# First group's up products as seven products of quarters, with weight sums kept in DRAM

## The chip, the cores and the metric

The kernel runs on one core of a Trainium2 chip. The metric is the device time of one execution in microseconds. TensorE (PE in the profile) multiplies, VectorE (DVE), ScalarE (ACT) and GpSimd (POOL) do the elementwise work, and SyncE (SP) issues most of the DMAs. Each engine runs its own instruction list in order; they wait for each other by semaphores (`x.wait_ge(sem, n)`, `.then_inc(sem, k)`). SBUF and PSUM tensors have 128 partitions.

## The reference

One inference step of a one-layer decoder, in fp32: 1024 prompt tokens with 16 meta tokens ahead of them, and 8 sequences of 8 new tokens over 8192 cached ones (1104 rows in all). Two branches run side by side, an RWKV-7 recurrence and sparse attention whose keys an indexer picks (the best 256 per query). Their outputs are gated and projected, and a convolutional FFN follows:

```python
def conv_ffn(h, conv_prev, lp):
    u = h @ lp['w_up']                     # 1024 -> 2 x 2816
    a, b = u[..., :D_FF], u[..., D_FF:]
    ext = jnp.concatenate([conv_prev.astype(a.dtype), a], axis=1)
    c = lp['conv_b'] + ext[:, 0:T] * lp['conv_w'][0]
    for j in range(1, CONV_W):             # CONV_W = 3
        c = c + ext[:, j:j + T] * lp['conv_w'][j]
    y = (jax.nn.gelu(c, approximate=False) * b) @ lp['w_down']
    return y, ext[:, T:]
```

`h` is the RMS-normed row of the residual stream. For the new tokens the indexer's top 256 of 8200 scores per query are needed before their attention can run.

## The kernel before

The program runs in stages: `project_attention` (attention inputs, blocks of 128 rows), `prompt_and_project` (prompt attention beside the RWKV projection), `sample_scores`, the RWKV factors and chunks, and `tail`, in which the change mostly lies. `tail` keeps rows as columns: the 1104 rows are three groups g = 0, 1, 2 of 368 columns (W), with the 1024 features in 8 tiles (KD) of 128 partitions. Each group goes through branch (16 products), project (8), up and down.

*Up and down of groups 0 and 1.* For each of 22 tiles f (NF) of the FFN width, `up(g, f, j)` makes `a` (j = 0) and `b` (j = 1): 8 matmuls each of a 128x128 weight with XN's 368 columns, into three PSUM banks in turn (R0, R1, R2), each given back through `freed`. ScalarE's `read_a` reads `a` with the three taps of the convolution, `read_b` copies `b`; GpSimd adds the taps (`conv_add`), ScalarE does the gelu (`curve`), and GpSimd multiplies by `b` into HT (`gate_up`). Then `down(g, t, h)` makes 8 output tiles t of 22 matmuls each, VectorE's `add_down(g, t)` adds a tile to X1 and frees its bank, ScalarE squares it, and TensorE's `sum_tile` sums the squares over partitions for the next norm. In group 0 `sum_tile(1, t - 1)` stands in TensorE's list right behind `down(0, t, 1)` for t from 1 to 7.

*The norm ahead of group 0's up products.* VectorE writes XN as X1 times the gain only (L2984). The first `a` and `b` are multiplied from it and are scaled afterwards by 1/RMS (`temper`, L2769), while GpSimd scales XN's eight tiles in place (L2629), each once TensorE's first `b` has read it.

*The top-k.* SC holds 4100 scores per partition (two halves of a query's scores in partitions p and p + 64). `topk(i)` is one of 96 steps of VectorE: MAX8, FIND_INDEX8, MATCH_REPLACE8 in turn, 32 rounds of 8. `steps(a, b)` does steps a to b - 1. They are spread through VectorE's list: 0 to 10 in group 0's branch and project, 11 and 12 around the reciprocal and the tempering, 13 to 61 during group 0's up products, 62 to 77 between its `add_down`s, 78 to 95 in group 1.

*The new tokens' attention.* In group 1 `lists()` (VectorE) turns the top-k into cache rows, with small transfers by GpSimd behind block LISTED and LISTED + 1; TensorE flips the list ahead of block FLIP; GpSimd hands `conv_add` over to VectorE from block BY_POOL and starts 128 indirect loads of keys and values into KV; and 36 `slot(s)` pieces of attention run on TensorE, two per up block from F0 on and then three per down tile (at CUTS). SP waits for `summed`, which slot 34 completes, before it loads group 2's branch inputs into YT, which lies in KV's space.

*Group 2* uses another scheme for up and down (`block3`): the weight and the moving tile are cut into quarters (two halves of the contraction, and `a` and `b` of the weight, two halves of 184 columns), and seven products of quarters take the place of eight, Strassen's scheme in Winograd's form. It needs four sums of weight quarters, made by VectorE (`weight_sum`, L1983 to L1989), and four mixtures of quarters of XN (`mix_norm`, L2870 to L2878). The seven results are kept or added by ScalarE, VectorE and GpSimd.

*`project_attention`* works through nine blocks of rows: TensorE 32 matmuls (L148), ScalarE copies with scale (L180), VectorE `rope` (L202 and on) and `level` (L225), SP stores k, v and the index keys (L98).

## Time and profile before

| | us |
|---|---|
| median of three runs (lowest, highest) | 2738.84 (2736.39, 2741.65) |
| the profiled execution: its own time | 2747.19 |
| the profiled execution: span, first to last instruction | 2745.4 |
| TensorE busy in the span | 2612.7 (95%) |
| VectorE busy | 1675.1 (61%) |
| ScalarE busy | 765.2 (28%) |
| GpSimd busy | 331.3 (12%) |
| granted TensorE clock, mean | 0.967 |
| group 0's up products, about | 1475 to 1697 |
| group 0's down products, about | 1697 to 1810 |
| group 1's up and down products, about | 1900 to 2337 |
| group 2's seven-product blocks, from | 2431 |

In the profile PE is TensorE's matmuls and PEld its weight loads, which overlap them; a matmul of this kernel in fp32 is two instructions of each kind. "L2214" is line 2214 of the kernel. Times in the timelines are microseconds from the start of the span; a bracket behind a row is the idle time of the engine in front of it and what ended it. An average over the whole span hides that stages have different limits, so the stages around the change are read one by one.

### The profile page before, as it was taken

The page shows a single profiled execution, that of the slowest core. Times are in us where ns is not written, and L with a number is a line of the kernel's source. Part 1 is how long each engine was busy: PE and PEld are TensorE (multiplying, and loading weights), DVE is VectorE, ACT ScalarE, POOL GpSimd, SP SyncE. Part 2 cuts the span into 40 slices and gives each one's busy share as a digit, 9 for nine tenths or more (in the row PEclk, how much of TensorE's full clock was granted, in tenths as well). Part 3 has the DMA queues.
Part 4 walks back from the last instruction along what each step waited for, and adds up shares of the span by engine and source line. Part 5 has one row for each costly group of instructions (what it writes and reads, how often), then busy time and mean ns, then how long its engine had stood idle before and what let it go on. Part 6 is the DMA issues. An engine that isn't in the chain of part 4 may idle for free.

```text
span 2745.4 us, 47811 instructions
## 1 busy us (share of the span) xinstructions
PE 2612.7 (95%) x18832; PEld 1734.1 (63%) x18832; DVE 1675.1 (61%) x3223; ACT 765.2 (28%) x1624; POOL 331.3 (12%) x467
## 2 busy tenths in 40 slices
PE   8998999999997997899899999999999999999997
PEld 5553566666654323788755666655656666579997
DVE  2115888864533457667669999977853321357666
ACT  2224322125443663011112332012335421222212
POOL 0000111000000000000002222000344440011111
PEclk9999999999998986999899999999999999999999
DMA  6101112131113440000243333344356663433332
GB/s 219 34 13 41 41 67 85 67 101 37 49 49 125 176 145 16 5 26 12 91 131 114 107 107 114 105 149 141 111 175 210 191 206 109 151 126 123 124 123 72
DMA packets 86591, 280.52 MB, mean 102 GB/s; under 512 B 18520, under 2 KB 42936, under 8 KB 72992
## 3 DMA queue, kind: packets, MB, share of 16 engines
q1 hardware_dynamic: 74336, 226.34, 24.7%
q0 software_dynamic: 12032, 51.14, 5.8%
q8 instruction: 149, 2.44, 0.4%
q14 instruction: 74, 0.61, 0.1%
HBM read 244.48 MB, written 32.16 MB: 101 GB/s over the span
## 4 chain that ended last, share of the span: by engine, by line
PE 53%; DVE 3%; issue 1%; DVEq 1%; DMA 1%; ACT 0%; POOL 0%; ACTq 0%; POOLq 0%; SPq 0%
PE banks L2214 10%; PE banks L2253 6%; PE banks L2232 6%; PE tl_P L2214 5%; PE tl_P L2253 4%; PE rc_P L1366 3%; PE tl_P L2232 2%; PE banks L2146 2%; PE banks L2158 2%; PE banks L1378 1%; PE tl_P L2146 1%; PE rc_LV L1378 1%; PE tl_P L2311 1%; PE tl_P L2332 1%; PE tl_P L2158 1%
## 5 line engine op out<-in xcount | busy, mean ns | idle before, releaser
L408 PE MATMUL dp_PS<-base,dp_W 128*128 128x368 f32 x1440 | 465.8, 476 | 0.0
L408 PEld LDWEIGHTS dp_PS<-base,dp_W 128*128 128x128 f32 x1440 | 265.8, 190 | 157.5 <-issue 8.8
L2214 PE MATMUL banks<-base,tl_WU 128*128 128x368 f32 x944 | 299.9, 475 | 0.8 <-DVE base L2763 0.8
L2214 PEld LDWEIGHTS banks<-base,tl_WU 128*128 128x128 f32 x944 | 179.2, 191 | 113.2 <-issue 3.6
L148 PE MATMUL pa_PG<-pa_W,base 128*128 128x402 f32 (+1 forms) x576 | 198.6, 505 | 7.7 <-DMA pa_W<-in_w_dsa 7.7
L707 DVE TENSOR_SCALAR_CACHE_REDUCE dp_EQ<-dp_SCORE,dp_trial 128x1024 f32<-128x1024 f32 (+1 forms) x186 | 176.0, 946 | 19.9 <-issue 1.1
L148 PEld LDWEIGHTS pa_PG<-pa_W,base 128*128 128x128 f32 (+1 forms) x576 | 106.9, 187 | 94.4 <-issue 14.2
L2232 PE MATMUL banks<-base,tl_WD 128*128 128x368 f32 x484 | 153.5, 474 | 0.0
L2214 PE MATMUL tl_P<-base,tl_WU 128*128 128x368 f32 x464 | 151.2, 477 | 0.2
L2704 DVE MAX8 tl_v<-arena 128x8 f32<-128x4100 f32 x32 | 141.8, 4431 | 2.9 <-issue 1.1
L2707 DVE FIND_INDEX8 tl_i<-tl_v,arena 128x8 uint32<-128x4100 f32 x32 | 141.5, 4423 | 0.3 <-issue 0.3
L2710 DVE MATCH_REPLACE8 arena<-tl_v,arena 128x4100 f32<-128x4100 f32 x32 | 141.2, 4414 | 0.0
L2654 POOL DMA_INDIRECT arena<-in_cache_kv,tl_PHT x128 | 123.3, 963 | 110.0 <-PE tl_P L2332 73.9
L2232 PEld LDWEIGHTS banks<-base,tl_WD 128*128 128x128 f32 x484 | 90.8, 190 | 57.2 <-issue 2.9
L2214 PEld LDWEIGHTS tl_P<-base,tl_WU 128*128 128x128 f32 x464 | 87.6, 191 | 58.1 <-POOL base L2629 4.3
L2427 ACT ACTIVATE arena<-base 128x368 f32<-128x368 f32 x44 | 22.1, 509 | 273.1 <-DVEq L2747 109.8
L202 DVE TENSOR_TENSOR pa_t<-pa_H,pa_cs 128x168 f32<-128x168 f32 (+1 forms) x9 | 3.0, 334 | 147.5 <-ACT pa_H L180 147.5
L785 DVE CUSTOM_DVE_ANT_0 dp_P<-dp_PS,dp_SCORE 128x1024 f32<-128x1024 f32 (+7 forms) x64 | 48.5, 758 | 66.7 <-PE dp_PS L458 59.1
L2158 PE MATMUL banks<-base,arena 128*128 128x368 f32 x256 | 81.3, 473 | 2.2 <-issue 1.4
L2146 PE MATMUL banks<-arena 128*128 128x368 f32 x240 | 77.3, 473 | 1.6 <-DMA arena<-in_wb 0.8
L2394 POOL TENSOR_TENSOR base<-tl_T 128x368 f32<-128x368 f32 x34 | 28.7, 843 | 400.9 <-ACTq L2477 400.8
L2232 PE MATMUL tl_P<-base,tl_WD 128*128 128x368 f32 x220 | 69.8, 474 | 0.0
(500 smaller groups left out, 4608.5 us busy)
## 6 DMA issues: line engine op xcount, KB each, us to landing
tl_WU<-in_wu SPq DMA_DIRECT2D x58, 1024.0 KB, 4.9
tl_WD<-in_wd SPq DMA_DIRECT2D x32, 704.0 KB, 4.2
dp_W<-in_w_rw SPq DMA_DIRECT2D x15, 1024.0 KB, 5.1
arena<-in_wb SPq DMA_DIRECT2D x24, 512.0 KB, 3.8
arena<-in_wo SPq DMA_DIRECT2D x24, 512.0 KB, 3.8
gates<-dp_PX SPq DMA_DIRECT2D x16, 552.0 KB, 3.6
arena<-gates SPq DMA_DIRECT2D x48, 184.0 KB, 3.9
arena<-in_wu SPq DMA_DIRECT2D x8, 1024.0 KB, 4.9
```

The source lines that it names most:

```text
L148: last = pe.matmul(PG[0:n, c, 0:NC4], xT[:, k, r:r + n], W[:, c, k, :], start=k == 0, stop=k == KD - 1)
L408: last = pe.matmul(bank(f)[:, 0:w], W[:, t // 2 % 2, k, 128 * (t % 2):128 * (t % 2) + 128], xT[:, k, c:c + w], start=k == 0, stop=k == KD - 1)
L707: dve.tensor_scalar(EQ[0:n, 0:m], scored_of(j), values(n, x), None, op, ALU.add, accum_out=result[0:n, x:x + 1])
L2146: last = pe.matmul(out[:, 0:W], WM[:, i % 2, o:o + 128], YT[:, j, k, :], start=k == 0, stop=k == 3)
L2158: last = pe.matmul(out[:, 0:W], WM[:, i % 2, 128 * k:128 * k + 128], MT[:, k, :], start=k == 0, stop=k == KD - 1)
L2214: last = pe.matmul(out[:, 0:W], WU[:, i % 2, o:o + 128], XN[:, k, :], start=k == 0, stop=k == KD - 1)
L2232: last = pe.matmul(out[:, 0:W], WD[:, i % 3, 128 * e:128 * e + 128], HT[:, f, :], start=f == 0, stop=f == NF - 1)
L2253: last = pe.matmul(out[:, 0:H], weights[:, k, :], moving(k), start=first and k == 0, stop=k == kk - 1, skip_group_check=True)
L2654: pool.indirect_dma_start(out=KV[:, n % 16, t, :], out_offset=None, in_=I["cache_kv"], in_offset=bass.IndirectOffsetOnAxis(ap=PHT[:, 64 * ...
L2704: dve.max(v8[:, :], SC)
L2707: dve.max_index(i8[:, :], v8[:, :], SC)
L2710: dve.match_replace(SC, v8[:, :], SC, TAKEN)
```

## The change

*In `project_attention`* SP loads each of the 22 up weights (1 MB), VectorE makes the four sums of its quarters in one to three tiles per row block, and SP writes them to a DRAM tensor `wsum` (1 MB per tile). ScalarE's squares are written over their input, which frees the room of `junk`.

*In group 0* only tile f = 0 is still made by `up`. Tiles 1 to 21 are made by `up_block(f)`: seven products of four matmuls of 184 columns into banks FA, FB, FD and FE, with weights from WU and, newly loaded for each tile, from WF (the sums out of `wsum`). ScalarE copies each result out of its bank (`keep`), seven per tile, and applies the taps from AF in SBUF; GpSimd makes the five additions between the parts and still does `conv_add` and `gate_up`. VectorE scales XN's low four tiles, GpSimd the high four; VectorE makes the four mixtures (XF) and only then does `steps(11, 62)`, where steps 11 and 12 were ahead of or between the reciprocal and the temperings.

*In group 1* BY_POOL, LISTED, FLIP and F0 are each two blocks later, so that 12 slots run in the up and 24 in the down products, and `sums` of the third norm waits for the last slot. Buffers, semaphore counts and the order of banks are adapted.

```diff
+                    for f in ups_of(b):
+                        sp.wait_ge(pair_summed, f + 1)
+                        sp.dma_start(wsum[f], WS[:, f % 2].rearrange("p e n -> p (e n)")).then_inc(ws_out[f % 2], 16)
+                        if f + 2 < NF:
+                            load_up(f + 2)
...
+                def sum_up(f):
+                    q, s = WQ[:, f % 2], WS[:, f % 2]
+                    dve.wait_ge(wq_in[f % 2], 16 * (f // 2 + 1))
+                    if f >= 2:
+                        dve.wait_ge(ws_out[f % 2], 16 * (f // 2))
+                    dve.tensor_tensor(s[:, 0], q[:, 2], q[:, 3], ALU.add)
+                    dve.tensor_tensor(s[:, 2], q[:, 0], q[:, 2], ALU.subtract)
+                    dve.drain()
+                    dve.tensor_tensor(s[:, 1], s[:, 0], q[:, 0], ALU.subtract)
+                    dve.drain()
+                    dve.tensor_tensor(s[:, 3], q[:, 1], s[:, 1], ALU.subtract)
+                    dve.drain().then_inc(pair_summed, 1)
...
                     if b:
                         level(b - 1)
+                    for f in ups_of(b):
+                        sum_up(f)
                 level(NB - 1)
...
-BY_POOL, LISTED, FLIP, F0 = 12, 3, 12, 14
+BY_POOL, LISTED, FLIP, F0 = 14, 5, 14, 16
...
                 order += [("rows", g - 1, i) for i in range(6)]
             if g < 2:
-                order += [(x, g, f) for f in range(NF) for x in "ab"] + [("down", g, t) for t in range(KD)]
+                order += [(x, g, f) for f in range(NF if g else 1) for x in "ab"] + [("down", g, t) for t in range(KD)]
...
-                    if i >= 2:
-                        sp.wait_ge(b_done, i - 1)
+                    if i == 2:
+                        sp.wait_ge(b_done, 1)
+                    elif 2 < i < NF + 2:
+                        sp.wait_ge(fd_made, 2 * (i - 2))
+                    elif i >= NF + 2:
+                        sp.wait_ge(b_done, i - NF)
                     sp.dma_start(WU[:, i % 2, :], I["wu"][:, i % NF]).then_inc(wu_in[i % 2], 16)
...
+                def load_sums(f):
+                    if f == 1:
+                        sp.wait_ge(branched, 16)
+                        sp.wait_ge(merged, 16)
+                    if f >= 3:
+                        sp.wait_ge(fd_made, 2 * (f - 2))
+                    sp.dma_start(WF[:, f % 2].rearrange("p e k m -> p (e k m)"), wsum[f]).then_inc(wf_in[f % 2], 16)
...
+                    if g == 0:
+                        load_sums(1)
+                        load_sums(2)
...
+                            if g == 0 and f >= 3:
+                                load_sums(f)
...
+                    if n == 3:
+                        pe.wait_ge(y_done, TS // 4)
...
-                        if j == 0 and f == (1 if g == 0 else 0):
+                        if j == 0 and f == 0 and g:
...
+                    def product(out, weights, moving, first):
+                        for k in range(4):
+                            if f == 1 and moving is left:
+                                pe.wait_ge(xn_done, 2 * k + 2)
+                            last = pe.matmul(out[:, 0:H], weights[:, k, :], moving(k), start=first and k == 0,
+                                             stop=k == 3, skip_group_check=True)
+                        return last
...
+                    def second():
+                        pe.wait_ge(fb_taken, 2 * f - 2)
+                        if f == 1:
+                            pe.wait_ge(xf_done, 2)
+                        product(FB, ws[:, 1], lambda k: XF[:, 1, k, :], True).then_inc(fb_made, 1)
...
+                    left = lambda k: XN[:, k, half[0]]
+                    pe.wait_ge(wu_in[f % 2], 16 * (f // 2 + 1))
+                    pe.wait_ge(wf_in[f % 2], 16 * ((f + 1) // 2))
+                    pe.wait_ge(fa_taken, 2 * f - 2)
+                    product(FA, raw[:, 0], left, True).then_inc(fa_made, 1)
+                    if f > 1:
+                        second()
+                    pe.wait_ge(fd_taken, 2 * f - 2)
...
+                    product(FD, ws[:, 0], lambda k: XF[:, 0, k, :], True).then_inc(fd_made, 1)
+                    if f == 1:
+                        pe.wait_ge(freed[FREED_B], uses0[FREED_B])
+                        second()
+                    pe.wait_ge(fa_taken, 2 * f - 1)
+                    if f == 1:
+                        pe.wait_ge(xn_high, 4)
+                    product(FA, raw[:, 1], lambda k: XN[:, 4 + k, half[0]], False).then_inc(fa_made, 1)
+                    if f == 1:
+                        pe.wait_ge(xf_done, 4)
+                    pe.wait_ge(fb_taken, 2 * f - 1)
+                    product(FB, ws[:, 2], lambda k: XF[:, 2, k, :], False).then_inc(fb_made, 1)
+                    pe.wait_ge(fe_taken, f - 1)
+                    product(FE, raw[:, 3], lambda k: XF[:, 3, k, :], True).then_inc(fe_made, 1)
+                    pe.wait_ge(fd_taken, 2 * f - 1)
+                    product(FD, ws[:, 3], lambda k: XN[:, 4 + k, half[1]], False).then_inc(fd_made, 1)
...
-                    for f in range(NF):
+                    if g == 0:
+                        up(0, 0, 0)
+                        up(0, 0, 1)
+                        pe.wait_ge(freed[FREED_A], uses0[FREED_A])
+                        for f in range(1, NF):
+                            up_block(f)
+                        pe.wait_ge(fa_taken, 2 * NF - 2)
+                        pe.wait_ge(fb_taken, 2 * NF - 2)
+                        pe.wait_ge(fd_taken, 2 * NF - 2)
+                        pe.wait_ge(fe_taken, NF - 1)
+                    for f in range(NF if g else 0):
...
+                def keep(part, bank, made, taken, count):
+                    act.wait_ge(made, count)
+                    act.activation(part, bank[:, 0:H], ACT.Copy).then_inc(taken, 1)
...
+                def taps(f):
+                    s = f % 2
+                    w0, w1, w2, cb = (cw[:, k, f:f + 1] for k in range(4))
+                    if f >= 2:
+                        act.wait_ge(convolved, f - 1)
+                    act.wait_ge(f_right, f)
...
+                    act.activation(T[:, s, 0, 0:W], AF[:, s, 0:W], ACT.Identity, bias=cb, scale=w0)
...
+                    act.activation(AL[:, f, :], AF[:, s, W:W + 2], ACT.Copy)
+                    act.drain().then_inc(a_read, 1)
+
+                def keep_block(f):
+                    s = f % 2
+                    if f >= 3:
+                        act.wait_ge(b_read, f - 1)
+                    keep(f1[:, s, :], FA, fa_made, fa_taken, 2 * f - 1)
+                    if f > 1:
+                        taps(f - 1)
+                    keep(f6[:, s, :], FB, fb_made, fb_taken, 2 * f - 1)
+                    keep(f5[:, s, :], FD, fd_made, fd_taken, 2 * f - 1)
+                    keep(AF[:, s, 2:2 + H], FA, fa_made, fa_taken, 2 * f)
+                    keep(f7[:, s, :], FB, fb_made, fb_taken, 2 * f)
+                    curve(0, f - 1)
+                    keep(f4[:, s, :], FE, fe_made, fe_taken, f)
+                    keep(f3[:, s, :], FD, fd_made, fd_taken, 2 * f)
...
-                for k in range(KD):
+                for k in range(4, KD):
                     if k < KD - 1:
                         pool.wait_ge(gain_read, k + 1)
                     else:
                         pool.wait_ge(b_done, 1)
-                    pool.tensor_tensor(XN[:, k, :], XN[:, k, :], RS[:, :], ALU.mult).then_inc(xn_done, 1)
-                for f in range(NF):
-                    conv_add(pool, 0, f)
-                    if f:
-                        gate_up(pool, 0, f - 1)
+                    pool.tensor_tensor(XN[:, k, :], XN[:, k, :], RS[:, :], ALU.mult).then_inc(xn_high, 1)
+                def finish_up(f):
+                    s = f % 2
+                    pool.wait_ge(fd_taken, 2 * f)
+                    pool.tensor_tensor(AF[:, s, 2 + H:2 + W], f16[:, s, :], f3[:, s, :], ALU.add).then_inc(f_right, 1)
+                    pool.tensor_tensor(BC[:, s, half[1]], f167[:, s, :], f5[:, s, :], ALU.add)
+                    pool.wait_ge(fe_taken, f)
+                    pool.tensor_tensor(BC[:, s, half[0]], f167[:, s, :], f4[:, s, :], ALU.add)
+                    pool.drain().then_inc(b_read, 1)
+
+                for f in range(1, NF):
+                    s = f % 2
+                    if f > 1:
+                        finish_up(f - 1)
+                    pool.wait_ge(fa_taken, 2 * f - 1)
+                    pool.wait_ge(fb_taken, 2 * f - 1)
+                    pool.tensor_tensor(f16[:, s, :], f1[:, s, :], f6[:, s, :], ALU.add)
+                    conv_add(pool, 0, f - 1)
+                    gate_up(pool, 0, f - 1)
+                    pool.wait_ge(fb_taken, 2 * f)
+                    pool.tensor_tensor(f167[:, s, :], f1[:, s, :], f7[:, s, :], ALU.add)
+                    pool.drain()
+                finish_up(NF - 1)
+                conv_add(pool, 0, NF - 1)
...
-                    dve.tensor_tensor(TX[:, 2], high[:, :, half[1]], low[:, :, half[1]], ALU.subtract).then_inc(tx_done, 1)
+                    if first_group:
+                        temper("b", b_done)
+                        dve.wait_ge(xn_high, 4)
+                    dve.tensor_tensor(to[:, 1], high[:, :, half[1]], to[:, 0], ALU.subtract).then_inc(done, 1)
+                    dve.tensor_tensor(to[:, 2], high[:, :, half[1]], low[:, :, half[1]], ALU.subtract).then_inc(done, 1)
                     dve.drain()
-                    dve.tensor_tensor(TX[:, 3], high[:, :, half[0]], TX[:, 1], ALU.subtract).then_inc(tx_done, 1)
+                    dve.tensor_tensor(to[:, 3], high[:, :, half[0]], to[:, 1], ALU.subtract).then_inc(done, 1)
...
                     if g == 0:
-                        steps(11, 12)
                         dve.wait_ge(rooted, 1)
                         dve.reciprocal(RS[:, :], RS[:, :])
                         dve.drain().then_inc(inverted0, 1)
                         temper("a", a_done)
-                        steps(12, 13)
-                        temper("b", b_done)
-                        steps(13, 62)
+                        for k in range(4):
+                            dve.wait_ge(gain_read, k + 1)
+                            dve.tensor_tensor(XN[:, k, :], XN[:, k, :], RS[:, :], ALU.mult).then_inc(xn_done, 2)
+                        mix_rows(XF, xf_done, True)
+                        steps(11, 62)
```

## Rows read from the trace of the kernel before

**Rows 1.** The profile's page, part 4: the chain by engine.

```profile
PE 53%; DVE 3%; issue 1%; DVEq 1%; DMA 1%; ACT 0%; POOL 0%; ACTq 0%; POOLq 0%; SPq 0%
```

**Rows 2.** Busy us of PE, PEld, DVE, ACT, POOL; clock; DMA share, GB/s.

```profile
1475.00:1697.00 222.00, 221.64 (x711) 134.06 (x710) 217.83 (x116) 72.90 (x179) 65.91 (x73) 1.00 0.30 105
```

**Rows 3.** Groups by line, VectorE, 1483 to 1697 (busy us, mean ns).

```profile
L2704 DVE MAX8 tl_v<-arena 128x8 f32<-128x4100 f32 x16 | 70.9, 4432 | 1.1
```

**Rows 4.** Timelines of TensorE and VectorE (start us, us, engine line operation).

```profile
1696.75 13.77 PE L2232 MATMUL tl_P<-base,tl_WD 128*128 128x368 f32 x44
...
1739.08 13.77 PE L2232 MATMUL tl_P<-base,tl_WD 128*128 128x368 f32 x44
...
1717.86 0.54 DVE L2746 TENSOR_TENSOR base<-base,tl_P 128x368 f32<-128x368 f32 x1
...
1737.13 0.54 DVE L2746 TENSOR_TENSOR base<-base,banks 128x368 f32<-128x368 f32 x1
```

**Rows 5.** Chain that ended last, in order of time (start us, us).

```profile
1494.10 9.89 PE banks L2214 x32
...
2441.86 2.49 PE tl_P L2253 x16
```

**Rows 6.** Timelines of TensorE and GpSimd at the head of the up products.

```profile
1479.34 7.58 PE L2214 MATMUL banks<-base,tl_WU 128*128 128x368 f32 x24
1486.86 7.25 PE L2214 MATMUL tl_P<-base,tl_WU 128*128 128x368 f32 x16
...
1485.75 7.41 POOL L2629 TENSOR_TENSOR base<-base,tl_RS 128x368 f32<-128x368 f32 x8 [90.57 <-PE banks L2214]
```

**Rows 7.** Timeline of VectorE at the same place.

```profile
1478.54 4.41 DVE L2710 MATCH_REPLACE8 arena<-tl_v,arena 128x4100 f32<-128x4100 f32 x1
...
1483.19 2.45 DVE L2997 RECIPROCAL tl_RS<-tl_RS 128x368 f32<-128x368 f32 x1
...
1490.72 0.55 DVE L2769 TENSOR_TENSOR banks<-banks,tl_RS 128x368 f32<-128x368 f32 x1
```

**Rows 8.** Timeline of VectorE, last group's mixtures.

```profile
2433.18 0.93 DVE L2875 TENSOR_TENSOR arena<-base,arena 128x736 f32<-128x736 f32 x1
...
2435.04 0.93 DVE L2878 TENSOR_TENSOR arena<-base,arena 128x736 f32<-128x736 f32 x1
```

**Rows 9.** Timelines of VectorE and GpSimd in the second group.

```profile
2008.55 1.10 DVE L2798 TENSOR_TENSOR arena<-arena 128x128 f32<-128x128 f32 x1
...
2012.25 0.29 DVE L2798 TENSOR_TENSOR arena<-arena 128x128 f32<-128x128 f32 x1
...
2008.54 0.96 POOL L2396 TENSOR_TENSOR base<-base,tl_T 128x368 f32<-128x368 f32 x1
```

**Rows 10.** Busy time and clock (columns as rows 2), and TensorE's timeline.

```profile
2044.00:2046.00 2.00, 2.00 (x7) 1.48 (x6) 0.00 (x0) 1.55 (x4) 1.63 (x2) 0.50 0.97 385
...
2043.13 1.88 PE L2311 MATMUL tl_P<-ident,arena 128*128 128x128 f32 x8 [2.61 <-DMA arena<-in_cache_kv,tl_PHT]
2044.80 6.02 PE L2214 MATMUL tl_P<-base,tl_WU 128*128 128x368 f32 x16
```

**Rows 11.** Groups by line and form, last group, 2430 to 2600.

```profile
L1985 DVE TENSOR_TENSOR arena<-arena,tl_WU 128x512 f32<-128x512 f32 x13 | 9.0, 692 | 1.2
...
L2682 POOL TENSOR_TENSOR base<-arena 128x184 f32<-128x184 f32 x14 | 8.0, 573 | 121.7 <-DVE arena L2926 121.7
...
L2524 ACT ACTIVATE arena<-banks 128x184 f32<-128x184 f32 x19 | 6.0, 318 | 27.0 <-PE banks L2253 26.7
```

**Rows 12.** DMA issues, 1475 to 1697 and 2300 to 2420 (KB, us to landing).

```profile
tl_WU<-in_wu SPq DMA_DIRECT2D x20, 1024.0 KB, 4.8
tl_WD<-in_wd SPq DMA_DIRECT2D x3, 704.0 KB, 7.4
...
arena<-ya_dram SPq DMA_DIRECT2D x1, 608.0 KB, 7.5
```

**Rows 13.** Timeline of VectorE in the attention projection.

```profile
101.78 0.33 DVE L202 TENSOR_TENSOR pa_t<-pa_H,pa_cs 128x168 f32<-128x168 f32 x1 [19.14 <-ACT pa_H L180]
```

More of the change, by code:

```diff
@@ L1963, in tail @@
         uses = [sum(1 for n in use.values() if n % 3 == r) for r in range(3)]
+        uses0 = [sum(1 for n in use.values() if n % 3 == r and n <= use["b", 0, 0]) for r in range(3)]
         NBL = len(BLOCKS3)
@@ L3131, in program @@
                         ident)
[L3132 removed]
+        tail(nc, I, S, M, soon, gates, wsum, yr_dram, ya_dram, O["v"], O["conv"], O["y"], ident)
 def shape_constants():
```

74 lines of the change are left out of this document (54 added, 20 removed).

## The prediction, made before the changed kernel was built or run

> **What bounds the kernel now.** I read the chain of waits first, then the busy time by stretch, then each engine's timeline at the ends of that stretch. The chain names TensorE for most of the run [rows 1], and in the first group's up products (1475 to 1697) TensorE is busy 221.64 of 222 us, so that the stage looks like pure TensorE work. In the same row VectorE is busy 217.83 of 222 us [rows 2]. That is the top-k over the 4100 scores per partition: each of its 96 steps is one search of 4.4 us [rows 3]. The reader should see what these steps stand in front of. In VectorE's program steps 13 to 61 come ahead of `add_down(0, 0)` (L2743). TensorE's own waits are: `sum_tile(1, t - 1)` after each down tile t waits for the square of tile t - 1, and that waits for `add_down`. In the trace the first down product starts at 1696.75 and is done 13.6 us later, but its addition starts only at 1717.86, directly behind a search; the second starts at 1737.13, again behind searches, with its tile done at about 1724. TensorE starts down tile 3 at 1739.08 [rows 4], 1.95 us after that second addition, once its square and the sum of it are done. By its own pace (13.6 us a down tile of 22 matmuls, 0.62 us a sum of squares) it would have started 0.1 us sooner. So before the change the two engines arrive at this point together. From tile 3 on TensorE sets the pace (14.22 us a tile) and VectorE waits for it. The start of down tile 3 is the gate, and the time at which it opens is the later of two chains: TensorE's (up products, three down tiles, a sum) and VectorE's (51 search steps, two additions, four more search steps).
>
> **TensorE's chain gets shorter.** An up block is two products of 8 matmuls of 368 columns, 32 instructions (a matmul is two of them) in 9.89 us. The last group already has the seven-product block: 16 of its instructions, of 184 columns, take 2.49 us, and a block has 7 x 8 = 56 of them, 8.72 us [rows 5]. 21 blocks change: 21 x (9.89 - 8.72) = 24.6 us. Head and end: before, the second block waits about 2.1 us for GpSimd's scalings (7.25 us for 16 instructions that take 5.1 with the tail of the last) [rows 6]; after, it waits about 1.3 us for the second mixture and 0.5 us for the last banks to be kept. Sum: 24.9 us, so the up products end at about 1671.9 instead of 1696.75.
>
> **VectorE's chain gets longer.** Before, VectorE does step 11 (from 1478.5 to 1483.19), the reciprocal (2.45 us), the tempering of the first `a`, step 12, the tempering of `b` at 1490.72, and starts step 13 at 1491.2 [rows 7]. After, steps 11 and 12 move behind the new work. Their price: step 11 4.7 us, step 12 4.5 us (a search of 4.43 us [rows 3] and its overhead), together 9.2 us. The new work fills the place that they had, and a little more. Sums 6 and 7 of the squares do not move, so the root is ready near 1480.5; reciprocal to 1483.0; tempering `a` to 1483.5; four scalings at 0.46 to 0.55 us, the last not before 1484.3, when TensorE has read tile 3, end at 1485.0. Then mixture 0, a TENSOR_TENSOR of 128x736, 0.93 us [rows 8]. The next step must wait: mixture 1 needs the high half of XN, which GpSimd scales tile by tile behind TensorE's reads of `b` (tile 4 is read at 1484.95, tile 7 at 1486.86 [rows 6]). GpSimd's eight such scalings now take 7.41 us, 0.93 each [rows 6], so its four end at 1488.6 if nothing disturbs them. Three mixtures of 0.85 to 1.0 us follow: 2.8 us (from the second to the end of the fourth [rows 8]). Step 11 would start at 1491.5.
>
> One more term. A VectorE operation with two tensors in SBUF beside a GpSimd operation takes up to its partner's time more: the same 128x128 addition takes 0.29 us alone and 1.10 us at 2008.55, while a GpSimd addition runs [rows 9]. Mixture 0 and GpSimd's first scaling start within 0.1 us of each other, so I add one GpSimd operation, 0.9 us, bounds 0 and 1.9. Step 11 starts at 1492.5. The shift of the search chain is then 1492.5 + 9.2 - 1491.2 = 10.5 us, with bounds 9.6 and 11.5. The searches themselves (one input tensor) I leave at 4.43 us although GpSimd gets five more additions a block: 16 of them beside GpSimd's present work average 4432 ns [rows 3].
>
> [...]
>
> **Which chain wins.** TensorE now ends its second down tile at 1671.9 + 27.2 = 1699.1 and must stand still until the first addition, 1717.86 + 10.5 = 1728.4, has been squared: about 30 us idle. It finishes tile 2 near 1744 and waits again for the second addition, 1737.13 + 10.5 = 1747.6. The gate opens at 1739.08 + 10.5 = 1749.6. All of the 24.9 us are spent waiting, and 10.5 us are lost on top. What is late next is everything behind it, one to one, as TensorE is busy without a gap from there.
>
> **The clock.** In the second group TensorE waits 2.61 us for the first gathered keys. Behind that wait its granted clock is 0.50, the 1.2 GHz level, from 2044 to 2046, and the 16 instructions from 2044.80 take 6.02 us where such 16 take 5.1 [rows 10]. With the slow transposes ahead of them that wait cost some 1.5 us beyond its own length. The 30 us idle will do the same, but what it costs falls into the 4 to 5 us of slack ahead of the gate. The second wait, 2 to 5 us, stands right at the gate. I take 1.5 us for it, bounds 0 and 3.
>
> The Trainium skill, "TensorE: Matmul & The Clock Gate", Part 1, says that the array is throttled by default and that activity lifts it, so that idle time is paid for after it ends. The row from 2044 agrees. Without that rule my sum would be 1.5 us less.
>
> **What is hidden, and by what.** (1) The block's other engines have to keep TensorE's pitch only loosely: three down tiles and a sum before 1749.6 allow the up stage to last until about 1708, 10.4 us a block against 8.72. ScalarE per block: seven keeps of 0.32 us [rows 11], the taps and the gelu, some 5 us. GpSimd: five additions of 0.57 us [rows 11] beside its present three (0.84 to 0.97), 5.6 us. Each block now loads two times 1 MB; one lands in 4.8 us, three of 704 KB together in 7.4 us [rows 12]. All are below 8.7. (2) Attention projection: 22 sums of four TENSOR_TENSORs of 128x512 at 0.69 us [rows 11], three sums a block, 8.4 us, in a hole of 19.1 us [rows 13]. The third sum waits for a load that is issued after the first: about 3.8 + 7.4 + 2.8 = 14 us after the hole opens, 5 us before it closes. Cost nothing; if the cover were gone, TensorE's `turn` of each block would come late by the excess. On SP a block's output writes stay ahead of its sums, and the row load behind them has a block and more in hand. (3) Second group: list, flip and slots come two blocks later. GpSimd no longer stands at its list transfers until the last search is done, VectorE waits for those transfers instead, and the flip is two blocks, 19.8 us, later, so TensorE does not feel it. The 36 attention slots cost TensorE the same in the down stage as in the up stage. (4) The last slots end some 9.5 us (15 matmuls of 0.62 us) ahead of the end of the down stage. SP waits for slot 34 before it loads the branch inputs; the last of these needs 7.5 us [rows 12] and is issued 2 us after the first, just in time. Cost 0, bounds 0 and 4 us.
>
> **Sum.** +10.5 (VectorE's chain) + 1.5 (clock) = +12 us. The profiled execution spans 2745.4 us and took 2747.19; it would become 2759.2. It stands 8.35 us above the median of the runs shown, 2738.84, so the forecast for the median is 2750.8 us.
>
> **Rivals.** *TensorE sets the end* (the searches turn out not to stand in the way): then the gain comes through, 2738.84 - 24.9 = 2714 us. For it: the chain names TensorE everywhere [rows 1]. Against it: the additions at 1717.86 and 1737.13 stand directly behind searches [rows 4]. It would need VectorE to be 25 us earlier. Chance 0.07. *The block's ring is slower than 10.4 us*: a keep, an addition and a load that don't overlap as I think. It decides from 10.4 us a block on; at 11 us the gate opens 21 x 0.6 = 13 us later still, 2764 us. For it: keeps and taps are in one queue with crossed waits. Against: 5 and 5.6 us of work in 8.7. Chance 0.07. *The third weight sum overruns its hole*: if the write and the load together need 6 us more than I take, 1 us a block in 7 blocks and more; at 3 us a block, 21 us, 2772 us. Chance 0.04. *The chains cancel*: the added wait is as computed, but fewer idle microseconds elsewhere (the slots meet more cover in the down stage, the 2.61 us wait goes) give back 7 to 12 us; about 2741 us. Against: TensorE is busy without gaps in that stage. Chance 0.09. *My forecast*: 0.73.
>
> **How the numbers follow.** The forecast's own range is 2738.84 + 9 to + 19 us (lower: 9.6 with no clock loss and 0.6 us for the spread of a median; upper: 11.5 + 3 + 4), 2748 to 2758. For 8 in 10 I add the near halves of the cancelling case and of the slow ring: 2743 to 2762 us. A measurement tells 0.2%, 5.5 us, from no change. Faster 0.08, same 0.10, slower 0.82.
>
> **What would show it.** The first `add_down` of group 0 about 10 us later than 1717.86, with a search right in front of it; a TensorE gap of about 30 us behind the second down tile and a short one behind the third; up blocks every 8.7 us; step 11 starting near 1492; no gap longer than today's in the attention projection; the distance from down tile 3 to the end as before. An up stage that is short and a first addition that is no later than 1718 would prove me wrong, and so would up blocks over 10.4 us.

## The result

The changed kernel takes 2756.85 us (median of four runs, 2755.63 to 2758.95), the kernel before 2738.26 us beside it: ratio 1.0060, 95% interval 1.0047 to 1.0073. The two medians differ by 18.6 us; the ratio gives 16.4 us (12.9 to 20.0). On a second occasion the ratio was 1.0055 (1.0042 to 1.0068). The mean of the two is 1.0057, +15.7 us. The forecast was +12 us, 2750.8, with a range of 2743 to 2762.

The profiled execution of the changed kernel spans 2755.2 us. That is only 9.8 us more than the span of before, since before's profiled execution lay 8.9 us above its median and this one lies at its median. Two single executions are therefore not compared by their ends here, but stage by stage.

The page of the changed kernel, busy time of each engine and the chain by engine (part 1 and part 4):

```profile
PE 2587.2 (94%) x19336; PEld 1784.8 (65%) x19336; DVE 1738.1 (63%) x3313; ACT 786.1 (29%) x1704; POOL 390.5 (14%) x575
...
PE 43%; DVE 10%; DVEq 4%; issue 1%; DMA 1%; ACT 0%; POOL 0%; ACTq 0%; POOLq 0%; SPq 0%
```

TensorE has 25.5 us less to do, and the run is longer. The chain answers [rows 1]: there PE held 53% of the span and DVE 3%, now PE holds 43% and DVE 10%. VectorE's new share is the search chain of the first group, which the chain now follows from 1493 to 1731. Its busy time by stretch (columns: PE, PEld, DVE, ACT, POOL busy, clock, DMA share, GB/s) answers [rows 2]:

```profile
1478.00:1673.00 195.00, 193.31 (x1206) 188.68 (x1205) 187.10 (x105) 96.80 (x258) 116.89 (x169) 1.00 0.60 227
1673.00:1752.00 79.00, 45.16 (x138) 26.89 (x137) 77.32 (x43) 3.62 (x8) 4.84 (x7) 0.81 0.17 51
```

The up products end at 1673, and in the 79 us behind them TensorE is busy for 45 while VectorE is busy for 77. TensorE's timeline at the gate (start us, us, then the idle time before and what ended it), with VectorE's first two additions of the group, answers [rows 4]:

```profile
1673.89 13.84 PE L2292 MATMUL tl_P<-base,tl_WD 128*128 128x368 f32 x44 [0.57 <-issue]
1687.57 13.77 PE L2292 MATMUL banks<-base,tl_WD 128*128 128x368 f32 x44
1732.34 1.59 PE L2177 MATMUL tl_P<-arena,tl_ones 128*128 128x368 f32 x2 [31.00 <-ACT arena L2543]
1733.72 15.61 PE L2292 MATMUL banks<-base,tl_WD 128*128 128x368 f32 x44
1751.61 0.89 PE L2177 MATMUL tl_P<-arena,tl_ones 128*128 128x368 f32 x2 [2.27 <-ACT arena L2543]
1752.33 13.77 PE L2292 MATMUL tl_P<-base,tl_WD 128*128 128x368 f32 x44
...
1726.62 4.42 DVE L2881 FIND_INDEX8 tl_i<-tl_v,arena 128x8 uint32<-128x4100 f32 x1
1731.11 0.54 DVE L2920 TENSOR_TENSOR base<-base,tl_P 128x368 f32<-128x368 f32 x1
...
1750.38 0.54 DVE L2920 TENSOR_TENSOR base<-base,banks 128x368 f32<-128x368 f32 x1
```

TensorE stands still for 31.00 us behind its second down tile. The wait is booked to ScalarE's square (L2543), but that square waits for the addition at 1731.11, and the addition stands directly behind a search. All three times of [rows 4] are 13.25 us later: the first addition, the second and down tile 3 (1739.08 before, 1752.33 now).

### The profile page after: what moved, and what is told of

The parts are those of the page before. It is cut to its first block, busy times and chain, and to the rows that moved or that the text cites. A ratio compares the mean times of both kernels' runs of the same rounds, so it can differ in the third digit from the quotient of the medians.

```text
span 2755.2 us, 49283 instructions
## 1 busy us (share of the span) xinstructions
PE 2587.2 (94%) x19336; PEld 1784.8 (65%) x19336; DVE 1738.1 (63%) x3313; ACT 786.1 (29%) x1704; POOL 390.5 (14%) x575
## 4 chain that ended last, share of the span: by engine, by line
PE 43%; DVE 10%; DVEq 4%; issue 1%; DMA 1%; ACT 0%; POOL 0%; ACTq 0%; POOLq 0%; SPq 0%
PE banks L2359 6%; PE banks L2274 5%; PE banks L2292 5%; PE tl_P L2359 4%; DVE arena L2884 3%; DVE tl_v L2878 3%; DVEq L2882 3%; PE rc_P L1395 3%; PE tl_P L2274 2%; PE banks L2206 2%; PE banks L2218 2%; PE tl_P L2292 2%; PE banks L1407 1%; PE tl_P L2206 1%; PE tl_P L2417 1%
## 5 line engine op out<-in xcount | busy, mean ns | idle before, releaser
L162 PEld LDWEIGHTS pa_PG<-pa_W,base 128*128 128x128 f32 (+1 forms) x576 | 107.2, 187 | 94.7 <-issue 14.3
L2274 PE MATMUL banks<-base,tl_WU 128*128 128x368 f32 x496 | 158.8, 477 | 0.8 <-DVE base L2937 0.8
L2878 DVE MAX8 tl_v<-arena 128x8 f32<-128x4100 f32 x32 | 141.8, 4432 | 3.3 <-issue 1.5
L2274 PEld LDWEIGHTS banks<-base,tl_WU 128*128 128x128 f32 x496 | 94.4, 192 | 60.0 <-issue 3.6
L2543 ACT ACTIVATE arena<-base 128x368 f32<-128x368 f32 x44 | 22.1, 509 | 295.7 <-DVEq L2921 143.2
L2304 PE MATMUL banks<-arena 128*128 128x184 f32 x504 | 85.6, 319 | 1.4 <-DVE arena L3052 1.4
L2304 PEld LDWEIGHTS banks<-arena 128*128 128x128 f32 x504 | 80.0, 190 | 1.6 <-issue 1.6
L2274 PE MATMUL tl_P<-base,tl_WU 128*128 128x368 f32 x240 | 76.8, 473 | 0.0
L594 ACT ACTIVATE dp_PMT<-dp_PS,dp_rest 128x368 f32<-128x368 f32 x42 | 23.8, 568 | 164.8 <-PE dp_PS L437 164.8
```

Source lines behind the costliest of these rows:

```text
L162: last = pe.matmul(PG[0:n, c, 0:NC4], xT[:, k, r:r + n], W[:, c, k, :], start=k == 0, stop=k == KD - 1)
L2274: last = pe.matmul(out[:, 0:W], WU[:, i % 2, o:o + 128], XN[:, k, :], start=k == 0, stop=k == KD - 1)
L2304: last = pe.matmul(out[:, 0:H], weights[:, k, :], moving(k), start=first and k == 0, stop=k == 3, skip_group_check=True)
L2878: dve.max(v8[:, :], SC)
```

## The experiments

The kernels ran on five occasions, and the kernel before, which ran on each, took 2738.3, 2768.3, 2767.0, 2742.7 and 2763.4 us on them. So kernels of different occasions are compared only by their ratios to the kernel before. For the stages I use marks on VectorE, the reciprocals of the norms ahead of group 0's up products (A), behind its down products (B), ahead of group 1's up products (C) and behind its down products (D). A to B is the stage of the change. A to B and B to C hardly depend on the occasion (329.66 and 329.67 for the kernel before on two of them); C to D does.

| kernel | ratio (95%) | A to B | B to C | C to D |
|---|---|---|---|---|
| before | 1 | 329.66 | 82.44 | 445.04 |
| `before_again` | 1.0001 (0.9989 to 1.0013) | 329.67 | 82.44 | 468.63 |
| `before_2_more` | 1.0032 (1.0018 to 1.0046) | 338.24 | 82.44 | 465.62 |
| `before_12_fewer` | 0.9992 (0.9982 to 1.0003) | 329.40 | 82.44 | 444.90 |
| `sums_alone` | 0.9999 (0.9987 to 1.0011) | 330.44 | 82.44 | 468.48 |
| `later_lists_alone` | 0.9995 (0.9982 to 1.0007) | 329.68 | 82.44 | 467.30 |
| after | 1.0060 (1.0047 to 1.0073) | 344.66 | 82.44 | 443.39 |
| `after_again` | 1.0055 (1.0042 to 1.0068) | 343.99 | 82.45 | 465.55 |
| `after_3_fewer` | 1.0006 (0.9996 to 1.0017) | 330.71 | 82.44 | 468.72 |
| `after_12_fewer` | 0.9929 (0.9915 to 0.9942) | 308.21 | 82.43 | 467.27 |
| `after_sums_postponed` | 1.0003 (0.9993 to 1.0013) | 331.63 | 82.43 | 467.47 |
| `moved_searches` | 0.9945 (0.9928 to 0.9961) | 310.23 | 85.89 | 444.30 |
| `moved_postponed` | 0.9941 (0.9925 to 0.9957) | 308.06 | 85.89 | 443.32 |
| `moved_searches_2` | 0.9934 (0.9919 to 0.9948) | 308.93 | 82.44 | 469.36 |

(The reciprocal A itself stands 2.7 us earlier in the changed kernel, counted from TensorE's sum in front of it, since step 11 is no longer in front of it; so the 15.0 us from 329.66 to 344.66 are 12.3 us of later work.)

**Theory and rivals.** Theory: the gate is set by VectorE's search chain, and what TensorE saves is spent waiting at it. Rivals: the sums in the attention projection cost what the gate leaves open; the later lists and slots cost time; the up blocks of quarters are slow; TensorE sets the pace and the searches are cover.

**One part of the change alone.** `sums_alone` is the kernel before with the new `project_attention`, whose sums nobody reads:

```diff
-            project_attention(nc, I, xT, ident, T, O["k"], O["v"], O["ki"], S)
+            project_attention(nc, I, xT, ident, T, O["k"], O["v"], O["ki"], wsum)
```

> The kernel before with only the weight sums in the attention projection (loads, four VectorE operations per tile, writes); nobody reads them. My theory: they lie in VectorE's hole of 19 us per block, so +1 us (the trace of after is 0.7 us late at the end of that stage), 2738 to 2741 us. Rival, that the sums are the unexplained part of the change: the medians differ by 18.6 us, of which the later gate explains about 13, so that 5 to 9 us come from here: 2743 to 2747 us.

The ratio says -0.3 us, with an interval from -3.6 to +3.0. The rival of 5 to 9 us is out. The traces resolve smaller differences than that. One of the softmax reciprocals of the prompt attention, always the same one, stands at 860.12, 860.09, 860.08, 861.12 and 860.19 in the five kernels without the sums (mean 860.3), and between 861.38 and 863.06 in the nine with them (mean 862.3). So the kernels with the sums are some 2 us late by then, where I had 0. VectorE's timeline of a row block of the changed kernel shows that the hole itself holds as computed:

```profile
105.14 1.22 DVE L239 TENSOR_TENSOR base<-base,pa_PR 128x1024 f32<-128x1024 f32 x1
106.55 0.69 DVE L248 TENSOR_TENSOR pa_WS<-pa_WQ 128x512 f32<-128x512 f32 x1 [0.19 <-issue]
...
118.44 0.69 DVE L248 TENSOR_TENSOR pa_WS<-pa_WQ 128x512 f32<-128x512 f32 x1 [6.04 <-DMA pa_WQ<-in_wu]
...
125.52 0.33 DVE L216 TENSOR_TENSOR pa_t<-pa_H,pa_cs 128x168 f32<-128x168 f32 x1 [4.25 <-ACT pa_H L194]
```

The third sum waits 6.04 us for its load, and 4.25 us of waiting for ScalarE are still left in front of `rope` (L216). The 2 us are not in the blocks: TensorE starts the next stage at 223.97 on average with the sums and at 223.73 without (224.27 and 223.57 in the first traces). The rest comes up behind that, in three steps. About 1.0 us of it goes back to this place, in the timelines of VectorE, GpSimd and TensorE of the changed kernel:

```profile
503.79 2.04 DVE L755 TENSOR_SCALAR dp_step<-dp_count 128x7 int32<-128x7 f32 x1
...
503.78 2.03 POOL L685 TENSOR_TENSOR dp_PMT<-dp_PMT,dp_PX 128x1040 f32<-128x1040 f32 x1 [12.63 <-ACTq L603]
...
590.73 1.56 PE L487 MATMUL dp_PS<-base,QT 64*128 64x512 f32 x6 [1.59 <-DVEq L819]
```

In the kernel before, the same operation of 128x7 elements starts 0.5 us ahead of the GpSimd addition and takes 0.17 us, and the wait at the third row is 0.59 us. In all nine kernels with the sums, one of the small operations at this place (L755 or L757) starts with or just behind the addition and takes 1.83 to 2.04 us; of the five without them only `before_2_more` has it (2.03 us), and it is the one at 861.12. The other two steps are 0.35 us each: VectorE has short "issue" gaps in this stage (seven of 0.4 to 0.5 us, 3.1 us in all, in `before`; nine, 4.1 us, in `after`), and in the kernels with the sums they stand at other instructions of its list, two of them where TensorE waits for it. This is read from the 14 traces; no run was made to separate it.

`later_lists_alone` is the kernel before with the constants and the norm's wait:

```diff
-BY_POOL, LISTED, FLIP, F0 = 12, 3, 12, 14
+BY_POOL, LISTED, FLIP, F0 = 14, 5, 14, 16
...
+                    if n == 3:
+                        pe.wait_ge(y_done, TS // 4)
```

> The kernel before with only the four constants (list, flip, hand-over of conv_add and slots two blocks later) and the third norm's wait for the last slot. My theory: TensorE's work is the same and the pieces of attention cost the same beside up as beside down: 0, at most -2 us. Rival, that slots moved from the up to the down products or the later end of the slots cost time: +3 us and more (the branch inputs of the third group come late by up to 4 us).

-1.4 us (-5.0 to +1.9), and its stage C to D is 1.3 us shorter than that of `before_again`. After is 1.65 us shorter than before in the same stage. The price of 0 (at most -2) holds, and the rival is out.

**The kernel before again.** This run changes nothing.

> The kernel before, unchanged, as a kernel of its own: ratio 1.000. It tells what its profiled execution is worth: the one shown spans 2745.4 us, about 9 us more than its median allows. If that span was one slow execution, this one spans about 2736 to 2738; if the profile itself stretches this kernel, it spans 2745 again.

The ratio fits (1.0001), but neither expectation of the span does: the kernel before now takes 2768 us, and its span is 2766.7. A to C is as before, and C to D is 23.6 us longer. TensorE's timeline shows where (start us, us, idle time before):

```profile
2058.40 0.47 PE L2214 MATMUL banks<-base,tl_WU 128*128 128x368 f32 x1 [1.63 <-issue]
2059.83 0.47 PE L2214 MATMUL banks<-base,tl_WU 128*128 128x368 f32 x1 [0.96 <-issue]
2063.32 0.77 PE L2214 MATMUL banks<-base,tl_WU 128*128 128x368 f32 x1 [3.03 <-issue]
2065.42 0.77 PE L2214 MATMUL banks<-base,tl_WU 128*128 128x368 f32 x1 [1.33 <-issue]
```

For 19 us TensorE issues single matmuls with 0.4 to 3 us of "issue" between them, 15.3 us in all; over the whole stage the granted clock is at its 1.2 GHz level for 31 us, against 7 us in the first trace of before. The gaps start 26 us after GpSimd's first indirect load (22 to 28 us in the nine traces that have them). The kernels of three of the four later occasions have it, changed or not, and those of the fourth (`moved_searches`, `moved_postponed`, `before_12_fewer`) don't, nor do the first traces of before and after. So it belongs to the occasion and cancels in the ratios. As for the 8.9 us by which before's first profiled execution lay over its median, this run only shows that its own profiled execution lies at its median, with runs between 2762 and 2773. The cause of the 8.9 us stays open.

**VectorE's chain alone, in the kernel before.**

```diff
                     if i % 3 == 0:
+                        if i in (24, 27):
+                            dve.max(v8[:, :], SC)
+                            dve.drain()
                         dve.max(v8[:, :], SC)
```

> The kernel before with two more MAX8 searches (their results are those of the searches behind them) among the steps of the first group's up products, so that only VectorE's chain grows, by 2 x 4.6 = 9.2 us, and TensorE's work is the same. My theory: both chains arrive together before the change (TensorE 0.1 us sooner), so the time grows by the whole of it: +9 us, 2747. Rival, TensorE sets the pace there and the searches are cover: 0.

+8.9 us by the ratio (5.0 to 12.7), +8.57 by stage A to B. TensorE's work is that of before, and it waits in the same place as in the changed kernel:

```profile
1724.73 1.59 PE L2119 MATMUL tl_P<-arena,tl_ones 128*128 128x368 f32 x2 [3.52 <-ACT arena L2427]
1726.12 16.07 PE L2232 MATMUL banks<-base,tl_WD 128*128 128x368 f32 x44
1744.00 0.89 PE L2119 MATMUL tl_P<-arena,tl_ones 128*128 128x368 f32 x2 [1.81 <-ACT arena L2427]
1744.72 13.77 PE L2232 MATMUL tl_P<-base,tl_WD 128*128 128x368 f32 x44
```

The counterpart takes 54 us out of VectorE's chain, with this in `topk` (r is the round; steps 24 to 35):

```diff
+                    if 8 <= r < 12:
+                        if i % 3 == 2:
+                            dve.tensor_copy(VAL[:, 8 * r:8 * r + 8], v8[:, :])
+                            dve.tensor_copy(IDX[:, 8 * r:8 * r + 8], i8[:, :])
+                            dve.drain()
```

> The kernel before with four rounds of the top-k (steps 24 to 35) left out in the first group's up products, copies of the round before in their place. My theory: before the change TensorE's chain is only 0.1 us ahead of VectorE's at the gate, so taking 54 us from VectorE gives 0 to -2 us. Rival, the searches bounded the kernel before as well: -10 us and more.

-2.2 us (-4.9 to +0.8), and -0.26 in stage A to B. So before the change both chains arrive together: 9 us more of searches cost 9, 54 us less give almost nothing. TensorE's own pace would open the gate 0.26 us sooner, for 0.1 in the prediction (whose own rates, three tiles of 13.6 us and two sums of 0.62 us from 1696.75, give 1738.8, 0.3 us sooner).

**The changed kernel with a shorter search chain.** The same lines, for one round and for four; like `before_12_fewer`, these kernels leave out part of the top-k.

> The changed kernel as it is, beside the kernel before on this chip, on which the kernel before takes 2768 us: ratio 1.0068 (+18.6 us) if the whole of the measured difference belongs to the change; 1.0045 (+12.4 us), if the gate (down tile 3 starts 12.3 us later, less the 1 us that was there ahead of the stage, and at most 2 us elsewhere) is all of it.

> The changed kernel with one round of the top-k (steps 24 to 26: MAX8, FIND_INDEX8, MATCH_REPLACE8) left out in the first group's up products; the round's eight results are copies of the round before, so part of the top-k isn't computed. My theory: VectorE's chain sets the gate, so 13.5 us less than the changed kernel (3 x 4.6 us less 0.3 us for the copies that stay), the first addition at 1717.6 and down tile 3 at 1738.8. Rival, the up blocks of quarters, their copies or loads are what costs: no change, the same time as the changed kernel.

> The changed kernel with four rounds (steps 24 to 35, 54 us of VectorE) left out in the same way. My theory: from some 36 us on TensorE sets the pace again, so down tile 3 starts at about 1716.4 (down products from 1673.9, three tiles of 13.8 and two sums) instead of 1752.3, and the time is 36 us below the changed kernel, about 23 us below the kernel before; the rest of the 54 us becomes VectorE's waiting. If VectorE were the limit all along, -54 us; if it never was, 0.

Against `after_again`, which ran beside them, one round less gives 1.0055 - 1.0006 = 0.0049 of 2767 us, 13.6 us, and 13.3 in stage A to B; expected 13.5. Four rounds less give 34.9 us by the ratios and 35.8 in the stage; expected 36. In the latter TensorE runs through the gate at its own pace (sum at 1695.29, 27.3 us behind the first down tile, where the changed kernel has 58.4):

```profile
1668.00 13.84 PE L2292 MATMUL tl_P<-base,tl_WD 128*128 128x368 f32 x44 [0.57 <-issue]
1681.68 13.77 PE L2292 MATMUL banks<-base,tl_WD 128*128 128x368 f32 x44
1695.29 0.78 PE L2177 MATMUL tl_P<-arena,tl_ones 128*128 128x368 f32 x2
...
1710.13 13.77 PE L2292 MATMUL tl_P<-base,tl_WD 128*128 128x368 f32 x44
```

Against the kernel before, this stage is 21.45 us shorter, and 24.2 us with the 2.7 us by which A stands earlier. That is the saving on TensorE which the changed kernel does not get out: the up blocks are not slow.

**The wait itself.** VectorE's work stays, TensorE asks for the addition one tile later:

```diff
-                        if g == 0 and t >= 1:
-                            sum_tile(1, t - 1)
-                    sums(2 * g + 1, KD - 1)
+                        if g == 0 and t >= 2:
+                            sum_tile(1, t - 2)
+                    sums(2 * g + 1, KD - 1 if g else KD - 2)
```

> The changed kernel with the first group's sums of squares one down tile later in TensorE's list (the sum of tile t - 2 behind down tile t, the last two at the end). VectorE's work and order stay. My theory: TensorE then waits for the first addition (1731.1) ahead of down tile 3 and for the second (1750.4) ahead of tile 4, which it would reach at 1747 and a little: one tile of 14.2 us less, plus 0.6 us for one more sum at the end, -13.6 us. Rival, that the time is lost in the up products or in the clock and not at this wait: 0.

-14.4 us by the ratios, -12.4 in the stage. The 31 us of idle time become 16.74. With that the changed kernel is level with the kernel before (1.0003).

**A version that uses the gain.** If the searches stand in the way, those that are not needed yet should stand elsewhere. Of the 85 steps from step 11 on, 44 stay ahead of the first addition (51 before), 17 go between the additions (16) and 24 into the second group (18):

```diff
-BY_POOL, LISTED, FLIP, F0 = 14, 5, 14, 16
+BY_POOL, LISTED, FLIP, F0 = 14, 6, 14, 16
+AT_DOWN = (55, 58, 60, 63, 65, 68, 70, 72, 72)
+AT_BRANCH = {3: 72, 7: 73, 9: 74, 11: 75, 15: 76}
+AT_PROJECT = {0: 77, 1: 78, 3: 79, 4: 80, 5: 81}
...
-                        steps(11, 62)
+                        steps(11, 55)
...
-                            if t == 0:
-                                steps(62, 64)
-                            if t < KD - 1:
-                                steps(64 + 2 * t, 66 + 2 * t)
+                            steps(AT_DOWN[t], AT_DOWN[t + 1])
...
-                        steps(85, 96)
+                        steps(82, 96)
```

(and one step at each place of the two maps; the copy of the flipped list into PHT stands ahead of the last masks.)

> The changed kernel with all 96 search steps, but spread by what TensorE needs: 44 instead of 51 of the first group's steps ahead of its first addition, two or three between the additions (17 instead of 16), and six more in the second group (one in branch, two in project, three in the up products), with the list transfers of GpSimd one block later and the flipped list copied ahead of the masks. My theory: the first addition comes at about 1699 and TensorE is back at its own pace, so as after_12_fewer: 36 us less than the changed kernel, some 20 us less than the kernel before (ratio 0.993), if the second group's list is still in time (rows done at 2046, relative to the trace of after, flip at 2051.9). Rival: the searches are only moved in front of the attention's list, and what is won at the gate is waited for at the flip, at the branch or at the project products: 10 us and more of the 36 come back as such waits.

> The same with the first group's sums of squares one down tile later in TensorE's list. My theory: TensorE's own pace is the limit in both, so no difference, at most -1 us where an addition with three steps ahead of it came late, and +0.6 us for the one more sum behind the last tile. Rival: the additions are still late in moved_searches, then this is faster by up to 5 us.

0.9945 and 0.9941: 15 to 16 us below the kernel before, some 31 below the changed one by the ratios, instead of 36. Stage A to B is there in full (34.4 us shorter than after). The loss is in B to C, 3.45 us longer, which the rival had named in part: TensorE's waits in this stretch are

```profile
1821.14 2.74 PE L2209 MATMUL tl_P<-arena 128*128 128x368 f32 x8 [1.36 <-DVEq L2905]
1827.91 2.74 PE L2209 MATMUL banks<-arena 128*128 128x368 f32 x8 [1.56 <-DVEq L2905]
```

both in the stretch where the fifth step stands in the branch products, which the changed kernel doesn't have there. The list is in time (rows done at 2010, flip at 2016.8), and the slots' first wait is 3.7 us instead of 2.5. Postponing the sums makes no difference that can be measured by the ratio, as expected. The last run moves that one step:

```diff
-AT_DOWN = (55, 58, 60, 63, 65, 68, 70, 72, 72)
-AT_BRANCH = {3: 72, 7: 73, 9: 74, 11: 75, 15: 76}
+AT_DOWN = (55, 58, 60, 63, 65, 68, 70, 73, 73)
+AT_BRANCH = {3: 73, 7: 74, 11: 75, 15: 76}
```

> As moved_searches, with one of the five steps in the second group's branch products moved ahead of the first group's last addition, where VectorE waits 4.25 us for the last down tile. In moved_searches the branch step costs TensorE 2.9 us of waits for its banks (1.36 and 1.56) that the changed kernel doesn't have. My theory: these go, and the last addition comes 4.62 - 4.25 = 0.4 us late: -2.5 us, about 18 us below the kernel before (ratio 0.9935), and 82.8 us instead of 85.9 between the second group's two reciprocals. Rival, branch and project products are late because of the five steps in project: the 2.9 us only move there, no difference.

B to C is back at 82.44, and the ratio is 0.9934 (0.9919 to 0.9948), 18 us below the kernel before. It is the fastest of all kernels with the whole computation here, though its lead over `moved_searches` lies within the intervals and rests on the stage.

## Why the prediction was right

**The mechanism was right.** Both chains arrived together before (`before_2_more` +8.9, `before_12_fewer` nothing); the change shortens one and lengthens the other, and only the other counts. TensorE's own saving was 24.9 us forecast; the up stage ends at about 1673.3, and the run was 0.97 us late before the stage (the row of up products at 1479.34 in [rows 6] starts at 1480.31), so 24.4. The number, 12 us, was partly luck: three terms were off and mostly cancel.

**The shift of VectorE's chain: 10.5 forecast, 12.3 measured** (13.25 less the 0.97). Its head came out to 0.1 us. VectorE's timeline, beside [rows 7]:

```profile
1484.47 1.89 DVE L3178 TENSOR_TENSOR base<-base,tl_RS 128x368 f32<-128x368 f32 x4
1486.46 1.51 DVE L3047 TENSOR_TENSOR arena<-base 128x736 f32<-128x736 f32 x1
1488.07 0.55 DVE L2943 TENSOR_TENSOR banks<-banks,tl_RS 128x368 f32<-128x368 f32 x1
1490.68 0.93 DVE L3052 TENSOR_TENSOR arena<-base,arena 128x736 f32<-128x736 f32 x1 [2.06 <-POOL base L2784]
...
1493.38 0.08 DVE L2884 MATCH_VALUE_LOAD arena<-tl_v,arena 128x8 f32 x1
```

Step 11 starts at 1493.38, 1492.41 on the clock of before, and 1492.5 was forecast. The first mixture took 1.51 us where one of the same size alone takes 0.93 (L3052). The chain runs through GpSimd, though: its four scalings took 4.45 us for the 3.7 I had, so the exclusion term of 0.9 was 0.75 there.

The mis-sized term is the one that leaves the search steps at their price although GpSimd gets more additions. The searches are indeed unchanged (17 MAX8 of 4432 ns), but the two small copies at the end of each round grow. VectorE's groups from 1493 to 1731 (busy us, mean ns):

```profile
L2878 DVE MAX8 tl_v<-arena 128x8 f32<-128x4100 f32 x17 | 75.3, 4432 | 1.6 <-issue 0.4
L2886 DVE CAST arena<-tl_i 128x8 f32<-128x8 uint32 x17 | 4.5, 262 | 0.0
L2885 DVE COPY arena<-tl_v 128x8 f32<-128x8 f32 x17 | 3.9, 230 | 0.0
```

One of the long ones, in VectorE's and GpSimd's timelines (start us, us):

```profile
1511.64 0.81 DVE L2886 CAST arena<-tl_i 128x8 f32<-128x8 uint32 x1
...
1511.58 0.85 POOL L2510 TENSOR_TENSOR base<-tl_T 128x368 f32<-128x368 f32 x1
```

Before, the CAST took 158 to 167 ns in all 16 rounds. Now its median is the same, 165 ns, but the one at 1511.64 starts behind the start of a GpSimd addition and ends with it. The warning stood in the trace of before: there the COPY (163 ns in the median) was stretched three times, to 0.67, 0.56 and 0.31 us,

```profile
1528.07 0.67 DVE L2711 COPY arena<-tl_v 128x8 f32<-128x8 f32 x1
...
1527.74 0.96 POOL L2410 TENSOR_TENSOR base<-base 128x368 f32<-128x368 f32 x1 [0.24 <-issue]
```

and the 49 steps lost 1.0 us by it; in the changed kernel seven copies are stretched, and the 51 steps lose 2.9 us. GpSimd is busy for 117 of 195 us in this stage, against 66 of 222 before [rows 2]. From step 11 to the first addition the chain takes 237.73 us, and 51 steps at before's pace (226.7 us for 49) take 235.9: 1.85 us more, the difference of these two. With it the sum closes: 10.5 - 0.1 + 1.85 = 12.25. `after_again` has four stretched copies in place of seven, and its chain takes 237.09 us, 0.65 less, which is the difference of the two in stage A to B. The Trainium skill, page "SBUF — State Buffer", section "Who interferes with whom", says that copies and casts can enter a mode with both ports and then exclude GpSimd. These rows agree; the prediction weighed only operations with two inputs.

**The clock: 1.5 forecast, 0 measured.** Behind the 31 us of idle time the granted clock is at the 1.2 GHz level, and behind the second wait it is not (columns as above):

```profile
1734.00:1736.00 2.00, 2.00 (x4) 1.07 (x4) 2.00 (x1) 0.00 (x0) 0.00 (x0) 0.50 0.00 0
...
1753.00:1755.00 2.00, 2.00 (x8) 1.28 (x7) 2.00 (x1) 0.00 (x0) 0.00 (x0) 1.00 0.03 8
```

Down tile 2 takes 15.61 us instead of 13.77, and that is hidden, as forecast. Down tile 3, behind a wait of 2.27 us, takes 13.77: the loss that I took over from [rows 10], where a wait of 2.61 us had transposes ahead of it, does not come.

**The attention projection: 0 forecast, about 2 us measured** by the marks near 860. The third sum ends 14.9 us after the hole opens and 4.25 us before it closes, for 14 and 5 forecast; what costs is not that hole. I had no term for anything outside it, such as the small operations of the next stage that now meet a GpSimd addition (near 503, above).

**The second group: 0 forecast.** `later_lists_alone` and the stage C to D give 0 to -1.7 us. Group 2's handover: D to the next reciprocal is 83.5 before and 82.6 after (82.4 to 83.5 in all 14 traces), so the bound of +4 us was idle.

Sum: 12.3 + 2.0 = 14.3 us, against 15.7 from the ratios, whose interval is about 2.5 us to either side. The 12 us were two errors against each other (+1.8 and +2 too little, 1.5 too much). Of the rivals, the slow ring is out (8.73 us a block in the changed kernel), so is the overrunning third sum as a wait in its hole, and so is the cancelling case: the stages behind the gate give back 0 to 3 us, not 7 to 12.

## What to carry to other kernels

When two engines meet at one point of the program, a saving on one of them is worth nothing until the other's chain to that point is shorter too: before a change to the busier engine, follow the other one back from the meeting point and count what stands in its list only because there was room. Here the work in the way was not urgent, and moving it turned 16 us of loss into 18 us of gain with the same arithmetic. And when VectorE's fillers or copies stand on such a chain, each operation given to GpSimd beside them can have a price there.

## What the runs showed of the hardware

- A 128x8 CAST of 0.165 us took 0.81 us beside a GpSimd addition of 0.85 us, while searches of 4.42 us over 4100 elements did not change. An operation of 0.16 us can so cost five times its length, and only now and then: 7 of the 34 copies in the stage took over 0.35 us. A TENSOR_SCALAR of 128x7 elements took 2.04 us instead of 0.17 beside a GpSimd addition of 2.03 us.
- TensorE's clock: behind 31.00 us of idle time a down tile took 15.61 us, behind 16.55 us 15.76, and behind only 3.52 us (`before_2_more`) 16.07, all against 13.77. Behind 1.81, 2.13 and 2.27 us it took 13.77. The granted clock was 0.50, the 1.2 GHz level, behind the 31.00 us and behind the 3.52 us. The loss did not grow with the length of the wait.
- On three of five occasions TensorE had 14 to 16 us of "issue" gaps while indirect loads ran, with the granted clock at the 1.2 GHz level for 27 to 31 us of the stage (3 to 7 us on the other two), and the stage C to D was 20 to 26 us longer, in every kernel; on the others neither. What differs between these occasions the runs don't show.
